# The first norm and the first two weight tiles of an eight-stage transformer kernel: fp32 products of x, roots multiplied in behind them, and second-half sums at later steps

## The reference, cut to what matters

```
def _rms_norm(x, g):
    xf = x.astype(jnp.float32)
    y = xf * lax.rsqrt(jnp.mean(xf * xf, axis=-1, keepdims=True) + EPS)
    return (y * g.astype(jnp.float32)).astype(x.dtype)

def _swiglu(h, w_gu, w_down):
    gate, up = jnp.split(h @ w_gu, 2, axis=-1)
    return (jax.nn.silu(gate) * up) @ w_down

for l in range(DEPTH):        # DEPTH = 2, D_FF = 2816
    x = x + 0.5 * _swiglu(_rms_norm(x, ffn1_norm[l]), ffn1_w_gu[l], ffn1_w_down[l])
    x = x + _hybrid_mixer(_rms_norm(x, mix_norm[l]), ...)
    x = x + 0.5 * _swiglu(_rms_norm(x, ffn2_norm[l]), ffn2_w_gu[l], ffn2_w_down[l])
x = _rms_norm(x, final_norm)
for l in range(DEPTH):
    h = rmsnorm(x, norm_g[l])
    ...                        # four attention branches, gates, merge
    x = x + merged @ w_out[l]
return rmsnorm(x, final_norm_g)
```

## Time and profile before

| What | us |
|---|---|
| Median of 3 runs | 1537.79 (1537.47 to 1537.88) |
| The profiled execution, its own time | 1536.93 |
| Its span, first instruction to last | 1535.0 |
| PE busy | 1520.4 |
| First 16-bit product of F0 starts | 15.31 |
| First `step_both` of F0 starts | 25.79 |

### The profile page before, as it was taken

The page is one execution under the profiler, slowest core; times in us unless marked ns, Lnnn a source line. Parts: engine busy times, 40 slices in busy tenths (PEclk is TensorE's granted clock), DMA queues, the critical chain, the costliest instruction groups (busy, mean ns, idle before and its releaser), DMA issues.

```text
span 1535.0 us, 32326 instructions
## 1 busy us (share of the span) xinstructions
PE 1520.4 (99%) x13737; PEld 1182.3 (77%) x13739; DVE 605.2 (39%) x1473; ACT 475.9 (31%) x1245; POOL 1024.3 (67%) x557
## 2 busy tenths in 40 slices
PE   8999999999999999999999999999999999999998
PEld 6666788888666866669889966668888889888885
DVE  3332275335332333315834533224444434353432
ACT  3321163413231133204541332213443313343322
POOL 6977576566777677775666677774658665648663
PEclk9999999999999999999999999999999999999999
DMA  9656544546565565565445465554455564446451
GB/s 384 218 193 205 191 172 166 188 167 220 200 212 193 193 228 211 194 205 190 169 165 192 166 234 203 209 192 154 158 197 179 178 206 154 172 147 241 165 192 56
DMA packets 42624, 293.95 MB, mean 191 GB/s; under 512 B 4720, under 2 KB 5232, under 8 KB 8688
## 3 DMA queue, kind: packets, MB, share of 16 engines
q1 hardware_dynamic: 41616, 290.57, 53.9%
q10 hardware_dynamic: 864, 1.30, 0.2%
HBM read 290.81 MB, written 1.05 MB: 190 GB/s over the span
## 4 chain that ended last, share of the span: by engine, by line
PE 97%; DVE 2%; DMA 0%; issue 0%; ACT 0%; ACTq 0%; DVEq 0%
PE ps L720 25%; PE ps L614 15%; PE ps L615 15%; PE ps L616 15%; PE ps L721 13%; PE ps L633 2%; PE ps L635 2%; PE ps L634 2%; PE ps L800 1%; PE ps L806 1%; PE ps L792 1%; DVE ps L1538 1%; PE ps L790 0%; DVE hP L1543 0%; DMA xT<-in_x 0%; PE ps L764 0%
## 5 line engine op out<-in xcount | busy, mean ns | idle before, releaser
L584 POOL TENSOR_TENSOR w_low<-ring 128x1024 f16<-128x1024 f32 (+1 forms) x548 | 1018.8, 1885 | 487.2 <-DMA ring<-in_w 486.9
L614 PE MATMUL ps<-hP,ring 128*128 128x256 f16 (+1 forms) x1952 | 473.1, 257 | 0.2 <-DVE hP L1543 0.2
L615 PE MATMUL ps<-hP,ring 128*128 128x256 f16 (+1 forms) x1952 | 472.9, 257 | 0.0
L616 PE MATMUL ps<-hP,w_low 128*128 128x256 f16 (+1 forms) x1952 | 472.8, 257 | 0.0
L720 PE MATMUL ps<-hP,ring 128*128 128x512 f16 x1280 | 416.2, 379 | 0.0
L721 PE MATMUL ps<-hP,w_low 128*128 128x256 f16 x1280 | 348.9, 273 | 0.0
L720 PEld LDWEIGHTS ps<-hP,ring 128*128 128x128 bf16 x1280 | 125.2, 98 | 150.8
L614 PEld LDWEIGHTS ps<-hP,ring 128*128 128x128 bf16 x1952 | 191.7, 98 | 23.5 <-issue 6.5
L616 PEld LDWEIGHTS ps<-hP,w_low 128*128 128x128 f16 x1952 | 190.9, 98 | 15.6
L615 PEld LDWEIGHTS ps<-hP,ring 128*128 128x128 bf16 x1952 | 191.0, 98 | 15.3
L720 PE MATMUL ps<-work,ring 128*128 128x512 f16 x528 | 171.8, 379 | 0.0
(11 more groups left out here) (271 smaller groups left out, 1714.0 us busy)
## 6 DMA issues: line engine op xcount, KB each, us to landing
ring<-in_w SPq DMA_DIRECT2D x261, 1024.0 KB, 4.8
ring<-in_w SPq DMA_DIRECT2D x12, 512.0 KB, 3.7
con<-in_const SPq DMA_DIRECT2D x1, 2812.0 KB, 18.1
gm<-in_gm SPq DMA_DIRECT2D x2, 1024.0 KB, 17.2
ring<-in_w SPq DMA_DIRECT2D x2, 768.0 KB, 4.4
ring<-in_w SPq DMA_DIRECT2D x2, 560.0 KB, 4.7
ring<-in_w SPq DMA_DIRECT2D x2, 544.0 KB, 3.7
xT<-in_x SPq DMA_DIRECT2D x2, 256.0 KB, 4.3
```

The lines of the kernel that those rows point to most:

```text
L584: nc.gpsimd.tensor_tensor(w_low[:, c % SLOTS, a:b], ring[:, c % SLOTS, a:b], w_high[:, c % SLOTS, a:b], ALU.subtract).then_inc(split.by((c ...
L614: nc.tensor.matmul(bank, w_high[:, slot, a:a + m], rhs(k, 0), start=(k == 0), stop=False)
L615: nc.tensor.matmul(bank, w_high[:, slot, a:a + m], rhs(k, 1), start=False, stop=False)
L616: mm = nc.tensor.matmul(bank, w_low[:, slot, a:a + m], rhs(k, 0), start=False, stop=(k == kt - 1))
```

## The change

The tiles gate 0 and up 0 of F0 are now computed in fp32, from the weights as they landed and from `x_gained`, x times the gains, which POOL makes (four products of 128 x 512). Such a tile is one fp32 matmul a block k. PE issues them before, between and behind the sums and the spread of the first norm; DVE multiplies both results by the spread root afterwards. Chunk 0 holds only these two tiles and isn't split; chunk 1 holds gate 1 and up 1. The idle matmuls behind the first norm go, and of the first 38, 34 stay. Three pieces of x are asked for on SP's queue ahead of the weights, one on ACT's; the parameters are asked for after ACT's squares. The squares are added 512 wide in two steps.

Between stages, the sums of t = 1 stand after k = 2 (B0: 4, with the spread after 6), those of t = 0 after step 10 with the spread after 22 (before B0: 13 and 24; they were 13 and 25, before B0 23 and 33) where a feed-forward ends, and before B0 the last update of t = 1 comes one block k earlier on DVE and its squares on ACT.

```diff
 RAW_BANK = (5, 7)
-WARM = (38, 5, 12)
+WARM = 34
...
     for b, key in enumerate(first):
-        place[key] = [(k // 4, k % 4 * 4 * P + b * P) for k in range(DK)]
-    size, split, last = [SLOT, SLOT], [True, True], [(first[3], True), (first[3], False)]
+        place[key] = [(b // 2, (2 * k + b % 2) * P) for k in range(DK)]
+    size, split, last = [SLOT, SLOT], [False, True], [(first[1], False), (first[3], False)]
...
 NCHUNK = len(SIZE)
-SPLITS = [[(a, min(a + (HALF // 2 if c == 0 else HALF), n)) for a in range(0, n, HALF // 2 if c == 0 else HALF)]
-          if SPLIT[c] else [] for c, n in enumerate(SIZE)]
+SPLITS = [[(a, min(a + HALF, n)) for a in range(0, n, HALF)] if SPLIT[c] else [] for c, n in enumerate(SIZE)]
...
+        x_gained, e = area(8192, DK, T)
+        first_root, _ = area(e, T)
         first_sq, _ = area(16384, DK, T)
-        first_so_far = ps[:, 0, :].rearrange("p (n t) -> p n t", n=2)
+        first_so_far = ps[:, 5, :].rearrange("p (n t) -> p n t", n=2)
...
-        first_squared = signal("first_squared", (0, 2, 1))
+        first_gained = signal("first_gained", range(4))
+        first_squared = signal("first_squared", range(3))
         first_by_dve = signal("first_by_dve", (3,))
-        first_summed = signal("first_summed", (0, 2, 1))
+        first_summed = signal("first_summed", (1, 2))
+        first_rooted = signal("first_rooted", ("root", "gate", "up"))
...
                                  ).then_inc(slot_landed[c % SLOTS], 16)
-                for i in range(2):
+                for i in range(3):
...
             def _(pool):
+                pool.wait_ge(ident_landed, 16)
+                for i in range(4):
+                    pool.wait_ge(x_landed[i], 16)
+                    g = const("g_F0")[:, 2 * i:2 * i + 2].rearrange("p (n o) -> p n o", o=1).to_broadcast([P, 2, T])
+                    nc.gpsimd.tensor_tensor(x_gained[:, 2 * i:2 * i + 2, :], xT[:, 2 * i:2 * i + 2, :], g, ALU.mult
+                                            ).then_inc(first_gained.by(i), 1)
                 for c in range(NCHUNK):
                     for h, (a, b) in enumerate(SPLITS[c]):
-                        if c == 0 and b <= HALF:
-                            pool.wait_ge(first_landed, 16)
-                        else:
-                            pool.wait_ge(*chunk_landed(c))
+                        pool.wait_ge(*chunk_landed(c))
...
                     over_rows(ps[:, ROOT_BANK[t], 0:P], rcol[:, 1, t:t + 1]).then_inc(spread.by((s, t)), 1)
-                def first_tiles(s, keys):
+                def first_tiles(s, keys, bank=0):
                     for t in norm_spans(s):
                         for k in range(DK):
                             pe.wait_ge(*low.at((s, k, t)))
-                            for b, key in enumerate(keys):
+                            for b, key in enumerate(keys, bank):
                                 if (t, k, b) == (0, 0, 0):
                                     pe.wait_ge(*summed.at((s, 6, 1, STREAMS[s] - 1)))
                                 step(ps[:, b, span(t)], key, k, DK, lambda k, part: hP[:, k, part, span(t)], ends=(t > 0))
-                            if t == 0 and k == 1:
+                            if t == 0 and k == (4 if s == "B0" else 2):
                                 norm_sums(s, 1)
-                            if t == 0 and k == 4:
+                            if t == 0 and k == (6 if s == "B0" else 4):
...
                 def first_norm(s):
-                    idle_work(WARM[0])
+
+
+                    idle_work(WARM)
                     pe.wait_ge(*first_by_dve.at(3))
                     for i in range(2):
                         for t in range(TT):
                             nc.tensor.matmul(ps[:, 4 + 2 * t, T:T + 1], first_sq[:, 6 + i, span(t)], ones[:, 0:1],
                                              start=(i == 0), stop=False)
-                    pe.wait_ge(*first_summed.at(1))
-                    for t in range(TT):
-                        mm = nc.tensor.matmul(ps[:, 4 + 2 * t, T:T + 1], acc[:, span(t)], ones[:, 0:1], start=False, stop=True)
-                    mm.then_inc(stat_done.by((s, 2)), 1)
-                    idle_work(WARM[1])
-                    pe.wait_ge(ident_landed, 16)
-                    pe.wait_ge(*inverted.at((s, 2)))
-                    for t in range(TT):
-                        mm = over_rows(ps[:, ROOT_BANK[0], span(t)], rcol[:, 1, t:t + 1])
-                    mm.then_inc(spread.by((s, 2)), 1)
-                    idle_work(WARM[2])
+                    for k in range(DK):
+                        if k % 4 == 0:
+                            pe.wait_ge(*(chunk_landed(0) if k else (first_landed, 16)))
+                        pe.wait_ge(*first_gained.at(k // 2))
+                        for b, kind in enumerate(("gate", "up")):
+                            c, a = PLACE[s, kind, 0][k]
+                            mm = nc.tensor.matmul(ps[:, b, 0:T], ring[:, c, a:a + P], x_gained[:, k, :], start=(k == 0), stop=(k == DK - 1))
+                            if k == DK - 1:
+                                mm.then_inc(done.by((s, kind, 0)), 1)
+                        if k == 1:
+                            pe.wait_ge(*first_summed.at(2))
+                            for i in range(2):
+                                for t in range(TT):
+                                    mm = nc.tensor.matmul(ps[:, 4 + 2 * t, T:T + 1], first_sq[:, i, span(t)], ones[:, 0:1],
+                                                          start=False, stop=(i == 1))
+                            mm.then_inc(stat_done.by((s, 2)), 1)
+                        if k == 2:
+                            pe.wait_ge(*inverted.at((s, 2)))
+                            for t in range(TT):
+                                mm = over_rows(ps[:, ROOT_BANK[0], span(t)], rcol[:, 1, t:t + 1])
+                            mm.then_inc(spread.by((s, 2)), 1)
...
                 def ffn(s):
-                    first_tiles(s, [(s, "gate", 0), (s, "up", 0), (s, "gate", 1), (s, "up", 1)])
+                    if s == "F0":
+                        first_tiles(s, [(s, "gate", 1), (s, "up", 1)], 2)
+                    else:
+                        first_tiles(s, [(s, "gate", 0), (s, "up", 0), (s, "gate", 1), (s, "up", 1)])
                     for j in range(2, FK):
                         b = 2 * (j % 4)
                         if j >= 4:
                             pe.wait_ge(*silu_done.at((s, j - 4)))
+                        elif s == "F0" and b == ROOT_BANK[0]:
+                            pe.wait_ge(*first_rooted.at("root"))
...
                     last_tiles(s, "down", FK, lambda k, part: hidden[:, k, part, :],
-                               *((23, 33) if after(s) == "B0" else (13, 25)))
+                               *((13, 24) if after(s) == "B0" else (10, 22)))
...
                 def first_norm(s):
-                    for i in (0, 2, 1):
+                    for i in range(3):
                         act.wait_ge(x_landed[i], 16)
                         nc.scalar.activation(first_sq[:, 2 * i:2 * i + 2, :] if i else first_so_far, xT[:, 2 * i:2 * i + 2, :],
                                              ACT.Square).then_inc(first_squared.by(i), 1)
+                    act.dma_start(par[:, :], par_in).then_inc(par_landed, 16)
...
                         square(s, 6, 1)
-                        for k in range(1, 6):
+                        m = 5 if s == "B0" else 6
+                        for k in range(1, DK):
+                            if k == m:
+                                square(s, 7, 1)
                             high_part(s, k, 0)
-                        square(s, 7, 1)
-                        high_part(s, 6, 0), high_part(s, 7, 0)
...
                         b = 2 * (j % 4)
-                        if j < 2:
+                        if j == 0 and s == "F0":
+                            act.wait_ge(*first_rooted.at("gate"))
+                        elif j < 2:
...
                 act.dma_start(con[:, 0:P + DK], const_in[:, 0:P + DK]).then_inc(ident_landed, 16)
-                for i in range(2, 4):
-                    act.dma_start(xT[:, 2 * i:2 * i + 2, :], x_in[:, 2 * i:2 * i + 2, :]).then_inc(x_landed[i], 16)
-                act.dma_start(par[:, :], par_in).then_inc(par_landed, 16)
+                act.dma_start(xT[:, 6:8, :], x_in[:, 6:8, :]).then_inc(x_landed[3], 16)
...
                 def first_norm(s):
-                    dve.wait_ge(*first_squared.at(2))
-                    nc.vector.tensor_tensor(first_sq[:, 4, :], first_sq[:, 4, :], ps[:, 0, 0:T], ALU.add).then_inc(first_summed.by(0), 1)
-                    dve.wait_ge(*first_summed.at(0))
-                    chain.link(nc.vector.tensor_tensor(ps[:, 0, 0:T], first_sq[:, 5, :], ps[:, 0, T:2 * T], ALU.add))
-                    nc.vector.tensor_tensor(ps[:, 0, 0:T], first_sq[:, 4, :], ps[:, 0, 0:T], ALU.add).then_inc(first_summed.by(2), 1)
```

(27 more changed lines are left out.)

## The result

The changed kernel takes 1526.7 us (median of 4, 1526.6 to 1526.8); the kernel before took 1537.8 in the same job (1537.5 to 1539.4). The ratio is 0.9926, 95% interval 0.9913 to 0.9938. That is 11.1 us faster.

What follows compares the result with a forecast made beforehand. PE's work plus PE's gaps were taken to bound the kernel. Gains of 3.1 + 2.6 + 1.0 + 2.5 = 9.2 us cut the span from 1535.0 to 1525.8; 1.93 around it and 0.86 gave 1528.6, range 1526.9 to 1531.8.

Steps and rivals of the forecast that it cites:

- The start: PE's work before the first `step_both`: start at 22.7 instead of 25.79, gain 3.1 us, between 2.6 and 3.8.
- K: When the first fp32 product may begin at the start: 9.0 us, between 8.3 and 9.5.
- Between stages: Moved sums and spreads remove PE's waits: 2.6 us in A0, F2, A1, 1.0 in F1, F3, B1, 2.5 in B0.
- B0's 2.5 us: In B0, earlier sums and spread remove 2.98 us of waits, less a new wait of 0.5.
- The other six places: Between stages outside B0: 2.6 us in A0, F2 and A1 together, 1.0 in F1, F3 and B1 together.
- The new wait for DVE's first low part: In B0, PE waits 0.5 us for DVE's first half-row of t = 1 behind the spread.
- The step from span to median: Whole kernel: 0.86 us added, as the earlier median lay that far above its profiled execution.
- (a): At the start, half clock over the fp32 products costs about 1.7 us, giving 1530.3; chance 0.25.
- (b): At the start, first weights land late behind x: 2 us more, giving 1530.6; chance 0.10.
- (c): Between stages, above all B0, a new wait replaces removed ones: 2 to 3 us not gained, 1531.1; chance 0.10.
- (d): DVE's rows end the start and sums follow DVE's add: 0 gained there, 2.0 between stages, 1535.8; chance 0.03.
- (e): PE at half clock from the start through all fp32 and 16-bit tiles makes it slower, 1542; chance 0.02.

Runs made afterwards that it cites:

- e7: Changed kernel with piece 2 of x on ACT's queue behind piece 3; 1526.9 us.
- e5: Changed kernel with 26 idle matmuls instead of 34 and POOL's second product waiting for DVE's square of piece 3; 1526.7 us.
- e15: Changed kernel with B0's steps and orders alone put back as they were before; 1529.1 us.
- e2: Changed kernel with the steps between stages as they were before, so only the start changed; 1534.9 us.
- e12: Kernel before with 62 instead of 38 idle matmuls, filling the gap ahead of the first sums; 1539.1 us.
- e1: Kernel before, unedited, profiled and timed again; 1537.7 us.
- e13: Kernel before with 62 instead of 38 idle matmuls at the start and 20 in B0's gap; 1536.2 us over 11 runs.
- e14: Kernel before with only B0's gap filled, by 20 idle matmuls; 1537.2 us.
- e6: Changed kernel without any idle matmuls; 1531.5 us.
- e4: Changed kernel with 26 idle matmuls instead of 34; 1527.5 us.
- e10: Changed kernel with 30 idle matmuls, POOL's second product after DVE's square, and constants asked for before chunk 5 instead of 3; 1526.2 us.
- e9: Kernel before with only the order of x changed: piece 2 on SP's queue ahead of the weights; 1538.6 us.
- e8: Changed kernel with B0's sums behind k = 3 and the spread behind k = 5; 1527.6 us.
- e3: Kernel before with only the changed steps between stages; 1530.7 us.

## Why the prediction was right, and where it was short

**The bound and the direction** were right: PE's work and its gaps are the time, and the gaps that the change closes come back in the span nearly to the forecast, 10.0 us for 9.2.

**The start.** PE's need from the first fp32 product to `step_both` was given as 13.67 us and measured 13.57 (8.42 to 21.99). By the distance of starts the 16 products took 7.07 us (forecast 6.96), the sums 0.81 (0.91), the spread 0.45 (0.56) and the rest 5.24 as forecast. K was mis-sized, 8.42 instead of 9.0. Of its terms the landing of piece 3 was off: it was put at 6.47, where piece 2 had landed, and it was there at 5.91. Why it came earlier is not shown; with a second piece behind it on ACT's queue (e7) DVE began at 6.11. The collision with POOL was predicted, and its size held: 1.45 us, where 1.1 to 1.8 behind the landing had been allowed. But the 0.95 us of the earlier trace rows, taken as the square's own length, already held a wait for POOL; its own length is 0.69. By the Trainium skill, SBUF — State Buffer, section "SBUF: two separate sides", a DVE operation with two SBUF inputs and a GpSimd one that reads SBUF hold each other off for the whole instruction. The runs agree: the square takes 0.69 us alone in e5 and 1.45 when a product of POOL began 0.14 us before it. That product ends at 6.81, and 0.69 more is 7.50, within 0.14 us of the square's measured end at 7.36. The gain at the start was 3.8, the upper bound that the prediction had for it, instead of 3.1.

**Between stages** 6.1 was forecast, 6.2 came. B0's 2.5 us stands: undoing B0 alone (e15) cost 2.4, by medians of different jobs. The other six places weren't undone one by one; their waits are gone from the list, and 6.2 less 2.4 leaves 3.8 where 3.6 was forecast. The new wait for DVE's first low part was 0.42, forecast 0.5.

**The step from span to median failed.** The prediction added 0.86 us because the median of before lay so far above its profiled execution, as if that belonged to every kernel. It belonged to the gaps. Behind B0's 2.42 us PE loses half its clock in some executions, 1.7 us each time (e2, e12, e15). Behind the start's gap it lost it in all five traces, and in three of them for so long that `step_both` came 1.6 to 2.6 us later, 1.05 of e1's 2.6 being the later sums. e13 shows the loss from the other side: with both gaps filled and nothing moved, the median falls by 2.2 us, of which at most 0.9 are an earlier `step_both`, and the spread by four fifths. How the 0.86 divides between the two gaps is not shown, since e12 and e14 don't add up to e13. The change removes both gaps, and with them this loss; the median of after lies 0.14 us below its profiled execution. 1.0 of the 1.9 us by which the forecast was too high is this term, 0.7 is the start (0.6 K, 0.1 the work behind it), 0.1 is between stages and 0.1 lies around the span. The prediction did read the half clock at the start, but counted it as lying where it hit nothing; it did not ask what it does in executions that weren't profiled, nor behind B0's gap.

**The bounds** of the forecast don't follow from its terms. With K at 8.3 and every gap gone the gain is 3.8 + 2.6 + 1.0 + 3.0 = 10.4 us, which gives 1527.4 and not 1527.8, and the low ends give 1530.4 and not 1530.2. The range's lower end, 1526.9, has no working. Had it been worked out without the 0.86, as the profiled execution itself, it would have reached down to 1526.5 and taken in the 1526.7.

**The rivals.** (a), half clock in the fp32 products, did not happen in the changed kernel, where 34 idle matmuls reach to the sums. But it is real: e5's longest execution shows it at its price of 1.7, and e6 at more. A gap ahead of the sums doesn't always bring it: in the traces of e4 (1.80 us) and e7 (0.81) the clock stays at 1.00. (b), late first weights, is refuted: the first product begins at 7.80 in e5 and at 7.81 in e10, so the first weights are there by then. (c) came at 0.42 us, already in the sum. (d) and (e) are refuted by the waits and by the clock.

**What stays open.** Why the same gap costs the clock in one execution and not in the next isn't shown by any trace here, nor why the half clock at the start lasts 3.4 us in one and 6.8 in another. In the six traces with B0's gap open, the three with the half clock at the start (before, e1, e9) have none in B0, and the three without it (e2, e12, e15) have it there; but four executions of e15 have a mean clock of 0.999 to 1.000, so one does not simply follow from the other. e4's long executions go with the clock (1528.4 at 0.998, 1531.7 at 0.996, the others at 0.999 and 1.000). Those of e8 (1527.2 to 1528.1 at 0.999 to 1.000) and e10 (1527.9 and 1530.2 at 0.999) show no such fall. None of them was profiled, and since e6's printed clock missed its half pace at the start, their cause stays open.

## What to carry to other kernels

A gap on PE costs its length, and in some executions the clock behind it as well. Where gaps can't be closed, idle matmuls in all of them took the scatter out here (e13); in one of two they did not (e12). If single times scatter, compare the profiled execution with the fastest, list the mean clock beside each time, look at the granted clock behind each gap, and don't carry the offset of a median over to a kernel that has other gaps. When a transfer takes another's place on a queue, give its landing a range: here it came 0.56 us earlier. And before an operation's time is used as its own length, see what ran beside it.

## What the runs showed of the hardware that was not expected

- The same wait of 2.42 us in B0 had clock 1.00 behind it in the traces of before, e1 and e9, and 0.50 for about 3.4 us in those of e2, e12 and e15.
- At the start the half clock behind the gap lasted 3.4 us in the traces of before and e14, and 6.8 us in those of e1, e3 and e9.
- 20 idle matmuls in B0's gap cost nothing measurable (PE still waits 0.24 us behind them in e13). With the start's gap filled too, eleven times spread over 1.1 us, against 5.5 for the kernel before.
- In e6, without idle matmuls, fp32 products took 0.89 us each at a granted clock printed as 1.00; at the same printed value the last ten took 0.45.
- A square of 128 x 512 by DVE takes 0.69 us alone and up to 1.49 beside POOL.
